# A reordered prologue of the combination, and 64-row expert tiles that transpose the next rows behind their last gate-up product

## The reference, cut to what matters

```python
# experts: each token goes to 4 of 32 experts
gu   = ragged_dot(xs, w_gu, group_sizes) + b_gu[sorted_e]      # 1024 -> 2048
act  = (up + 1.0) * (gate * sigmoid(1.702 * gate))             # clamped to +-7
y    = ragged_dot(act, w_down, group_sizes) + b_down[sorted_e] # 1024 -> 1024
h    = h + sum over a token's 4 experts of gate_weight * y
# combination
gate = sigmoid(rms_norm(h, norm_ple_w) @ ple_gate_w)           # 1024 -> 1024
h    = h + gate * (p @ ple_proj_w)
x    = rms_norm(h, final_norm_w)                               # end of block one
z    = rms_norm(x, pre_norm_g) @ w_in                          # 1024 -> 1984, block two
```

## Time and profile before

| what | us |
|---|---|
| median of 3 runs (lowest, highest) | 5306.43 (5306.38, 5306.79) |
| the profiled execution, its whole time | 5315.76 |
| its span, first to last instruction | 5314.0 |
| TensorE busy in the span | 5063.8 (95%) |
| VectorE, ScalarE, GpSimd busy | 3279.9, 2209.7, 627.2 |

### The profile page before, as it was taken

The page is one execution under the profiler, slowest core; times in us unless marked ns, Lnnn a source line. Parts: engine busy times, 40 slices in busy tenths (PEclk is TensorE's granted clock), DMA queues, the critical chain, the costliest instruction groups (busy, mean ns, idle before and its releaser), DMA issues. The chain is left out here.

```text
span 5314.0 us, 79004 instructions
## 1 busy us (share of the span) xinstructions
PE 5063.8 (95%) x25725; PEld 3510.6 (66%) x25726; DVE 3279.9 (62%) x6262; ACT 2209.7 (42%) x3349; POOL 627.2 (12%) x862
## 2 busy tenths in 40 slices
PE   7999999899999999999999999959998799999798
PEld 4666666566666666666666666636665688888465
DVE  5444454577777777777777777765557544444266
ACT  4222222454444445555555555433332533333254
POOL 0000000000000000000000000011010399200000
PEclk9999999899999999999999999979999999999899
DMA  8777777765565657777777777453342400000433
GB/s 286 238 242 248 237 253 197 234 195 191 181 204 170 207 163 235 236 242 239 242 238 239 237 239 233 164 185 128 137 141 83 149 7 7 7 7 7 150 102 101
DMA packets 426919, 929.83 MB, mean 175 GB/s; under 512 B 60720, under 2 KB 77552, under 8 KB 425968
## 3 DMA queue, kind: packets, MB, share of 16 engines
q1 hardware_dynamic: 364144, 766.01, 44.2%
q10 hardware_dynamic: 35328, 87.57, 4.9%
q0 software_dynamic: 27280, 74.02, 4.2%
HBM read 777.78 MB, written 151.78 MB: 175 GB/s over the span
## 5 line engine op out<-in xcount | busy, mean ns | idle before, releaser
L1447 DVE TENSOR_TENSOR w_lo_gate<-stage,w_hi 128x1024 bf16<-128x1024 f32 (+1 forms) x800 | 929.6, 1179 | 209.2 <-ACT w_hi L1311 151.5
L1311 ACT ACTIVATE w_hi<-stage 128x1024 fp32r<-128x1024 f32 (+1 forms) x800 | 790.5, 1016 | 529.5 <-PE GU L1135 283.7
L1132 PE MATMUL GU<-w_hi,x_hl 128*128 128x512 f32 x2048 | 852.0, 416 | 19.4 <-DVE x_hl L1452 10.5
L1133 PE MATMUL GU<-w_hi,x_hl 128*128 128x512 f32 x2048 | 803.3, 392 | 0.0
L1135 PE MATMUL GU<-w_lo_gate,x_bf 128*128 128x512 bf16 x2048 | 498.3, 381 | 0.0
L1132 PEld LDWEIGHTS GU<-w_hi,x_hl 128*128 128x128 f32 x2048 | 386.9, 189 | 130.6 <-issue 32.6
L1132 PE MATMUL Y<-w_hi,a_hl 128*128 128x512 f32 x1024 | 455.0, 444 | 1.7 <-DVE a_hl L1458 1.7
L1133 PEld LDWEIGHTS GU<-w_hi,x_hl 128*128 128x128 f32 x2048 | 387.3, 189 | 76.9
L1133 PE MATMUL Y<-w_hi,a_hl 128*128 128x512 f32 x1024 | 401.9, 392 | 0.0
L1135 PEld LDWEIGHTS GU<-w_lo_gate,x_bf 128*128 128x128 bf16 x2048 | 174.7, 98 | 251.3 <-issue 85.6
L2983 DVE TENSOR_REDUCE ntop<-SC 128x1 f32<-128x2048 f32 x64 | 146.7, 2292 | 266.1 <-PE SC L3096 266.1
(11 more groups left out here) (648 smaller groups left out, 9422.5 us busy)
## 6 DMA issues: line engine op xcount, KB each, us to landing
stage<-in_expert_w_gate_up_dram SPq DMA_DIRECT2D x512, 512.0 KB, 5.1
stage<-in_expert_w_down_dram SPq DMA_DIRECT2D x224, 512.0 KB, 6.5
stage<-w_in_lo SPq DMA_DIRECT2D x150, 512.0 KB, 5.8
stage<-in_w_out_dram SPq DMA_DIRECT2D x67, 512.0 KB, 4.6
expert_rows<-zero_y SPq DMA_DIRECT2D x64, 512.0 KB, 6.8
stage<-w_out_rows SPq DMA_DIRECT2D x64, 512.0 KB, 5.9
b_gu<-in_expert_b_gate_up_dram ACTq DMA_DIRECT2D x128, 256.0 KB, 4.6
expert_rows<-acted ACTq DMA_DIRECT2D x64, 512.0 KB, 3.3
```

What stands on the lines that cost most here:

```text
L1132: pe.matmul(out, high(k), w_high(k), start=(k == first), stop=False)
L1133: pe.matmul(out, low(k), w_high(k), start=False, stop=False)
L1311: act.activation(w_hi[:, c, ks, :], staged, ACT.Copy).then_inc(s["hi_done"], 1)
L1447: dve.tensor_tensor(w_lo[:, c, ks, :], staged, w_hi[:, c, ks, :], ALU.subtract).then_inc(s["lo_done"], 1)
```

## The change: what it does

In tiles of 64 rows TensorE's `transpose_rows(g + 1)` moves from behind the third `transpose_act` to directly behind the last gate-up product, and the third `transpose_act` moves ahead of `down_both(1)`. Tiles of 128 rows keep their order.

In the combination, half n of `w_in_2` becomes block n % 8 of rows, and columns 0 to 1023 for n < 8, columns 1024 to 1983 for n >= 8. The slots on `stage` lie 1024 words apart, and `tanh` moves behind them. TensorE's Z products 0 and 1 of tile 0 wait for 8 low parts, Z products 2 and 3 for 16. The orders of SP, ScalarE and VectorE in the prologue change as the diff shows. `low_hT(t)` is taken out of `scale_of(t)` and called by itself; in the steady loop it stands where it stood.

```diff
@@ tile() @@
+                if n < P:
+                    transpose_rows(g + 1)
                 pe.wait_ge(s["a_ready"], g * 6 + 2)
                 transpose_act(g, 1)
                 pe.wait_ge(s["y_taken"], g + 1)
...
                     down(1, 1)
+                    transpose_rows(g + 1)
                 else:
+                    transpose_act(g, 2)
                     down_both(1)
-                    transpose_act(g, 2)
-                transpose_rows(g + 1)
                 pe.wait_ge(s["a_ready"], g * 6 + 6)
@@ halves of w_in_2 @@
-HALF_Z = Z_COLS // 2
+HALVES_Z = ((0, 2 * BANK), (2 * BANK, Z_COLS))
...
-    return I["w_in_2"][0, n // 2 * P:(n // 2 + 1) * P, n % 2 * HALF_Z:n % 2 * HALF_Z + HALF_Z]
+    lo, hi = HALVES_Z[n // KD]
+    return I["w_in_2"][0, n % KD * P:(n % KD + 1) * P, lo:hi]
...
-        tanh = on_stage(S["stage"], 2 * Z_COLS, D)
+        tanh = on_stage(S["stage"], 8 * BANK, D)
@@ SP @@
             load(0, 0)
+            sp.wait_ge(s["y_in"], 16 * TOPK)
+            def load_raw(numbers):
+                for n in numbers:
+                    sp.wait_ge(s["proj_lo"], n - 3)
+                    sp.dma_start(raw_in(n), half_of_map(I, n)).then_inc(s[f"proj_in{n % 4}"], 16)
+
+            load_raw((4,))
+            sp.wait_ge(s["h_loaded"], 16)
+            load(1, 1)
+            load_raw((5, 6))
             load_pp(0)
             sp.dma_start(gain_final[:, :], ...).then_inc(s["gain_final_in"], 16)
-            sp.wait_ge(s["h_loaded"], 16)
-            load(1, 1)
-            for n in range(4, 2 * KD):
-                sp.wait_ge(s["proj_lo"], n - 3)
-                sp.dma_start(raw_in[n % 4], half_of_map(I, n)).then_inc(s[f"proj_in{n % 4}"], 16)
+            load_raw(range(7, 2 * KD))
             store_x2(0, 0, True)
@@ ScalarE: body() and prologue @@
                 if not is_step(t, 0):
                     copy_x2T(t - 1)
+                if is_step(t, 1):
+                    high_weights((13, 14, 15))
                 if has_this:
                     gate(t)
...
             copy_hT(1)
-            high_weights((9, 10))
+            high_weights((9,))
             square_3(0, 0)
+            high_weights((10,))
+            square_2(0, 0)
             high_weights((11, 12))
-            square_2(0, 0)
-            high_weights(range(13, 16))
             body(1, 1, True, True)
@@ VectorE: prologue @@
-            low_weights(range(4))
+            low_weights((0, 1))
             add_rows(0, 0)
+            low_weights((2, 3))
+            low_hT(0)
             low_weights((4,))
             scale_of(0)
             low_weights((5, 6, 7))
             add_rows(1, 1)
-            low_weights((8, 9))
             dve.wait_ge(s["gain_final_in"], 16)
-            finish(0, 0, False, ((10,), (11,)), False)
+            finish(0, 0, False, (lambda: (low_hT(1), low_weights((8, 9))), lambda: low_weights((10,))), False)
             scale_of(1)
-            low_weights(range(12, 16))
+            low_weights((11, 12))
+            low_x2(0)
+            low_weights((13, 14, 15))
             base = ch.n
-            low_x2(0)
             finish(1, 1, False)
+            low_hT(2)
             scale_of(2)
@@ TensorE: body() @@
-                if is_step(t, 1):
-                    pe.wait_ge(s["proj_lo"], 2 * KD)
                 for n, (lo, hi) in enumerate(Z_CHUNKS):
+                    if is_step(t, 1) and n % 2 == 0:
+                        pe.wait_ge(s["proj_lo"], (n // 2 + 1) * KD)
```

More of the change, by code:

```diff
@@ L1759, in raw_half @@
 def raw_half(stage, n):
-    return on_stage(stage, n % 4 * HALF_Z, HALF_Z)
+    lo, hi = HALVES_Z[n // KD]
+    return on_stage(stage, n % 4 * 2 * BANK, hi - lo)
 def half_of_map(I, n):
-    return I["w_in_2"][0, n // 2 * P:(n // 2 + 1) * P, n % 2 * HALF_Z:n % 2 * HALF_Z + HALF_Z]
+    lo, hi = HALVES_Z[n // KD]
+    return I["w_in_2"][0, n % KD * P:(n % KD + 1) * P, lo:hi]
 def is_step(t, n):
@@ L1836, in combine_phase @@
         Z = [pb("Z0", BANK), pb("Z1", BANK)]
-        raw_in = [raw_half(S["stage"], n) for n in range(4)]
-        half_of = lambda w, n: w[:, n // 2, n % 2 * HALF_Z:n % 2 * HALF_Z + HALF_Z]
+        raw_in = lambda n: raw_half(S["stage"], n)
+        half_of = lambda w, n: w[:, n % KD, HALVES_Z[n // KD][0]:HALVES_Z[n // KD][1]]
         names = """gain_ple_in gain_pre_in gain_final_in ident_ready gate_scaled gate_hi gate_lo pp_loaded hT_hi_ready proj_hi proj_lo y_seen y_used h_loaded h2_done hT_ps hT_sb
@@ L1998, in high_weights @@
                     act.wait_ge(s[f"proj_in{n % 4}"], 16 * (n // 4 + 1))
-                    act.activation(half_of(w_hi, n), raw_in[n % 4], ACT.Copy,
-                                   scale=gain_pre[:, n // 2:n // 2 + 1]).then_inc(s["proj_hi"], 1)
+                    act.activation(half_of(w_hi, n), raw_in(n), ACT.Copy,
+                                   scale=gain_pre[:, n % KD:n % KD + 1]).then_inc(s["proj_hi"], 1)
             def body(t, par, has_this, has_next):
@@ L2098, in scale_of @@
             def scale_of(t):
-                low_hT(t)
                 dve.wait_ge(s["sumsq_h"], t + 1)
@@ L2102, in scale_of, with finish @@
                 dve.tensor_scalar(rstd_h[:, :], rstd_h[:, :], 0.5, None, ALU.mult).then_inc(s["rstd_h_ready"], 1)
-            def finish(t, par, has_prev, meanwhile=((), ()), has_next=True):
+            def finish(t, par, has_prev, meanwhile=(None, None), has_next=True):
                 dve.wait_ge(s["tanh_done"], t + 1)
@@ L2111, in finish @@
                                          ALU.mult, ALU.add).then_inc(s["h3_done"], 1)
-                low_weights(meanwhile[0])
+                if meanwhile[0]:
+                    meanwhile[0]()
                 dve.wait_ge(s["sumsq_3"], t + 1)
@@ L2116, in finish @@
                                          ALU.mult, ALU.mult).then_inc(s["x2_done"], 1)
-                low_weights(meanwhile[1])
+                if meanwhile[1]:
+                    meanwhile[1]()
                 if has_next:
@@ L2138, in low_weights @@
                     dve.wait_ge(s["proj_hi"], n + 1)
[L2139 removed]
+                    dve.scalar_tensor_tensor(half_of(w_lo, n), raw_in(n), gain_pre[:, n % KD:n % KD + 1], half_of(w_hi, n),
                                              ALU.mult, ALU.subtract).then_inc(s["proj_lo"], 1)
@@ L2177, in _ @@
                     finish(i * 2 + u, u, True)
+                    low_hT(i * 2 + (u + 1))
                     scale_of(i * 2 + (u + 1))
@@ L2262, in _ @@
             finish(TILES - 2, 0, True)
+            low_hT(TILES - 1)
             scale_of(TILES - 1)
```

3 lines of the change are left out of this document (1 added, 2 removed).

## The result

The changed kernel takes 5269.56 us (median of 4, 5263.17 to 5271.47), the one before 5306.41 (5306.18 to 5306.79) in the same rounds: a ratio of 0.9929, 95% interval 0.9914 to 0.9943. That is 36.9 us less, with an interval of about 30 to 46. The forecast of 5265.7 is 3.9 us off and inside its range. As far as a time can tell, it was right; the trace shows that this is in part luck, since two errors cancel: the experts gave more than forecast, the prologue less.

A forecast was written before the change was run, and what follows sets the result against it. TensorE was taken as the bound, its idle time in 64-row tiles and prologue costing time; 19.2 + 21.5 = 40.7 us off the 5314 span gave 5273, and 5265.7 as median, range 5259 to 5281.

The forecast's parts named there:

- Part one: The 12 tiles of 64 rows: TensorE's new order wins 1.6 us a tile, 19.2 us in all, bounds 12 to 21.
- rival A: End of 64-row tiles: the wait on x_hl returns if the chain through the third transposes runs late; 5275, chance 0.12.
- C: 64-row tiles show no gain because the last tile behind each is bound by something else; 5285, chance 0.03.
- D: 64-row tiles: early row transposes wait for their gather, making the kernel slower, 5338 for a 20 us landing; chance 0.01.
- Part two: The combination's prologue: reordering brings turn(2) 21.5 us earlier, bounds 15 to 23.
- turn(0): Prologue: two low parts move behind add_rows(0), so it starts 3.4 us earlier, with 0 us taken for late rows.
- gate(0): Prologue: low_hT(0) runs beside the copies, so it starts 3.9 us after turn(0) and takes its 13.96 us.
- turn(1): Prologue: add_rows(1) 12.9 us behind turn(0), this turn 18.5 behind, using the old distances less low_hT's 0.89.
- rival B: Prologue turns to its transfers: late half 7 or gather slips add_rows(1) and all behind by 3 to 8 us; 5272, chance 0.13.
- gate(1): Prologue, largest piece: low_hT(1) follows tanh directly, so it starts 20.6 us earlier, 22.9 behind turn(0).
- Z: First Z product: 16.6 us after gate(1) starts, at the full clock; the low level would add 1.6 us.
- turn(2): Entry to the steady loop: set by VectorE, 56.7 us behind turn(0), with TensorE waiting 0.7; 21.5 us won.

The follow-up runs named there:

- experiment 4: Changed kernel with one move of the 64-row tiles undone: third transpose_act behind the second down product, 5291.37 us; or next rows turned at the tile's end, 5291.69 us.
- experiment 8: Changed kernel with pp and the final gain sent behind half 5, and half 8 held until tile 1's gather landed: 5266.94 us, ratio 0.9923.
- experiment 5: Changed kernel with low_hT(1) put back behind finish(0): 5281.82 us, ratio 0.9943.
- experiment 11: Changed kernel with pp and gain early, half 7 sent only after tile 1's gather landed, plus unread identity transposes in TensorE's idle time: 5267.19 us, ratio 0.9924.
- experiment 9: Changed kernel with unread identity transposes on TensorE around turn(0) and turn(1): 5267.83 us, ratio 0.9926.

## Why the prediction was right, and where not

**The bound** was read rightly. TensorE is the bound of the steady tile before and after (34.80 us, all busy), and what was won ahead of it stayed until its end: from turn(2) to the last transpose of x2 it is 503.5 us for 503.1, and 503.2 to 504.0 in the other twelve profiles.

**Part one** was right in kind and 2.6 us short. The step is the term of 1.6 us for a tile, which measured 1.78 in the first and 1.81 in the others. The room for x_low (0.3) was 0.15, so **rival A** was close but did not come. Its condition (a delay of the chain through the third TA) is what experiment 4 makes: with the third TA late, the wait on x_hl comes back in all twelve tiles, 6.3 us in total and up to 0.7 each. **Rivals C and D** did not occur: all twelve tiles show the gain, and no transpose of rows waits for its gather in the waits above.

**Part two** gave 17.3 us by turn(2) for 21.5, within its bounds of 15 and 23. By its steps:

- *turn(0)*, 3.4 earlier: right (3.3); tile 0's gather landed 5.7 to 6.4 us after issue, for 8.2 to 9.6 before; that this is because h(1), `pp` and the gain now stand behind it in SP's order is likely, and no run tests it. No cost, as taken.
- *gate(0)*, 3.9 behind turn(0): right.
- *turn(1)*: this is the step that failed. Low part 4 follows turn(0) by 6.0 us, as taken (5.97). But from it to `add_rows(1)` the prediction took the old order's 7.83 us less the 0.89 of low_hT, 6.9, and it is 10.8. The distance of the old order had no transfer in it that came late; here 2.5 us are VectorE's wait for ScalarE and half 7, and 1.0 its wait for the gather. The prediction left the transfers to rival B. `add_rows(1)` came 3.9 late. Experiment 8 shows the cause: with fewer bytes beside the gather it starts at 13.2, for the forecast 12.9.
- *gate(1)*: bound by turn(1) now, 3.5 us behind it, and not by tanh; so of the 3.9, 2.9 arrive. In experiment 8, where tanh does bind, it starts at + 22.9 as forecast. That its early start is on the path is shown by experiment 5.
- *Z*: I took the high clock and 16.6 us; it measured 17.2, and two errors hide in the 0.6 between them. The clock was not high: it went down to 0.50 and was back within gate(1), at 3492. The page "TensorE: Matmul & The Clock Gate" of the Trainium skill, Part 1, by which gate(1) would start cold, was right on this. And the high clock's value is not 16.6. That was the old 18.25 less 1.6, a price read off gate(0), while the old gate(1) took 14.9 us to the transposes of x2, for 12.1 with the clock high throughout (experiment 11); with the 3.3 from there to Z the high clock gives 15.4. So the low start cost 1.8 us in the changed kernel, for 2.9 before.
- *turn(2)*: I took 17.2 us behind Z, set by VectorE; it is 18.0, set by TensorE, which is busy throughout, at a clock of 0.63 until 3510. The low level at Z was in no step: in the profile before, the same gap of 2.26 us ahead of Z cost no clock. But the low level is not the new prologue's doing alone. It is in twelve of the fourteen profiles of this study, the tiles alone with the old prologue among them, with 18.0 to 18.1 us from Z to turn(2) in eleven of these; only the kernel before (16.5) and experiment 9 (17.0) kept the high one. In experiment 9 turn(2) waits 0.38 us for VectorE, which is the bound that I took, at nearly its value.

2.9 + 0.6 + 0.8 = 4.3 us, all of the difference between 56.7 and 61.0. The 0.6 at Z is itself what is left of 1.8 us for the clock and 1.2 the other way. **Rival B**, with 0.13, named the place and the engines (half 7, the gather, ScalarE, `add_rows(1)`), and its slip of 3 to 8 us was 3.9. It should have been the forecast: full queues were in the rows, and a step that issues the same bytes in less time keeps no distance measured before. The time hit because the experts gave 5.0 us more than taken, 2.6 of it in the tiles of 64 rows. The range covered both. A slip in the prediction's chances changes nothing: the forecast, A, B and C add to 0.99, and less 0.01 that is 0.98, not 0.97; nor does B's "at worst 5277", where a slip of 8 us gives 5274.

As to the rule of "SBUF — State Buffer" of the Trainium skill, Who interferes with whom, by which VectorE beside the gather would delay it by up to 1.25: the four issues of tile 1's gather take 1.16, 0.94, 0.94 and 0.94 us beside VectorE's low parts, and 0.96, 0.94, 0.94 and 0.94 in the kernel before, where VectorE stood idle; in both the first begins 1.0 us behind the copy that writes `slots`. At most 0.2 us can be put down to the rule here; whether issuing such a transfer is a read in the rule's sense no run shows.

## What to carry to other kernels

Where an order is tightened, the transfers in it get tightened too: count the bytes between the first issue and the last landing that is needed, and hold back what is needed later, since a queue that sends as soon as a slot is free fills every hole made for something else. A move on one engine is worth little while the engines that take its result have other work queued ahead of it; look at both orders, and move both or neither. And where the noise of a stage that isn't touched is as large as the effect, compare stretches between two events of the trace, not spans, and in more than one profile where a clock that falls or rises lies inside them.

## What the runs showed of the hardware

- A gather of 2 MB in four issues took 6.1 to 7.5 us from issue to landing beside 1 MB of other loads, and 7.5 to 11.9 where loads followed one another without end and the engines moved 384 GB/s over 15 us.
- TensorE's clock fell at short gaps, and not each time. In the changed kernel a gap of 3.64 us, a turn of 1.35 and a gap of 2.14 brought it from 1.00 to 0.50. The gap of 2.26 ahead of Z left it at 1.00 in the kernel before and brought 0.63 (over the 4.6 us behind it) in the changed one and in the tiles alone; in all three gate(1) began at the low level and ended at the high one. What decides this the rows here don't tell.
- Transposes of the identity, whose result nobody reads, were enough to bring the high level back: 44 of them ahead of turn(0) and 12 behind it gave a turn of 1.09 us for 1.94, and the 8 us of matmuls in gate(0) at 1.00. With 3.84 us of idle time behind 24 more, gate(1) still began at the low level; without that idle time (experiment 11) it ran at 1.00 for its 12.24 us.
- A product with the gate map took 12.1 to 12.2 us at the high level, and 12.5 to 15.0 with a start at the low one.
